# The MLP's down product by one level of Strassen's algorithm, with its weight side on GpSimd

## What is computed

```python
u = jnp.square(jax.nn.relu(_rms_norm(x, g_pre_ffn) @ w_up))
x = x + _rms_norm(u @ w_down, g_post_ffn)
```

## Time and profile before

| | us |
|---|---|
| median of 3 runs (2537.8 to 2539.58) | 2538.49 |
| the profiled execution, its own time | 2545.82 |
| its span, first to last instruction | 2544.0 |
| TensorE busy | 2479.0 (97%) |
| VectorE busy | 1157.3 (45%) |
| ScalarE busy | 674.2 (27%) |
| GpSimd busy | 491.4 (19%) |
| mean granted clock of TensorE | 0.987 |

### The profile page before, as it was taken

How to read it: one execution, slowest core, us unless ns; L and a number is a source line. 1 busy time by engine, 2 the same in 40 slices (tenths; PEclk the granted TensorE clock), 3 DMA queues, 4 the chain that set the end, 5 groups by cost and what they waited for, 6 DMA issues and landing times.

```text
span 2544.0 us, 37470 instructions
## 1 busy us (share of the span) xinstructions
PE 2479.0 (97%) x14264; PEld 2358.0 (93%) x14264; DVE 1157.3 (45%) x2297; ACT 674.2 (27%) x1365; POOL 491.4 (19%) x729
## 2 busy tenths in 40 slices
PE   6999999999999999999999999999999999999998
PEld 6999999999999999999999999988899898898996
DVE  4053424324276666566657435555343343333335
ACT  5222232323222222222222323333121131131221
POOL 1021211102164455445436000001000000000000
PEclk8999999999999999999999999999999999999999
DMA  4251625343333313313323633222021021110114
GB/s 150 90 191 64 225 81 196 103 166 117 121 102 124 117 66 132 123 65 119 127 88 113 216 125 130 93 99 85 17 67 39 27 66 33 33 58 25 50 41 157
DMA packets 219182, 256.88 MB, mean 101 GB/s; under 512 B 8256, under 2 KB 186816, under 8 KB 218944
## 3 DMA queue, kind: packets, MB, share of 16 engines
q1 hardware_dynamic: 219072, 255.37, 30.4%
HBM read 175.12 MB, written 80.22 MB: 100 GB/s over the span
## 4 chain that ended last, share of the span: by engine, by line
PE 72%; issue 12%; DVE 11%; DMA 2%; POOL 2%; ACT 1%; SPq 0%; DVEq 0%; POOLq 0%; ACTq 0%
PE bank L593 10%; PE bank L595 10%; PE bank L594 10%; PE bank L823 5%; PE bank L825 5%; PE bank L824 5%; PE bank L893 5%; PE bank L892 5%; PE bank L894 5%; PE bank L744 3%; DVE QE L1374 2%; DVE PP L1377 2%; PE bank L851 1%; PE bank L853 1%; PE bank L852 1%
## 5 line engine op out<-in xcount | busy, mean ns | idle before, releaser
L593 PE MATMUL bank<-XH,WHI 128*128 128x384 f32 x2304 | 792.9, 344 | 14.3 <-DVE WLO L1209 5.5
L595 PE MATMUL bank<-XH,WLO 128*128 128x384 f32 x2304 | 775.8, 337 | 0.0
L594 PE MATMUL bank<-XL,WHI 128*128 128x384 f32 x2304 | 775.6, 337 | 0.0
L593 PEld LDWEIGHTS bank<-XH,WHI 128*128 128x128 f32 x2304 | 437.6, 190 | 20.4 <-ACT ZST L908 7.1
L594 PEld LDWEIGHTS bank<-XL,WHI 128*128 128x128 f32 x2304 | 437.5, 190 | 0.9
L595 PEld LDWEIGHTS bank<-XH,WLO 128*128 128x128 f32 x2304 | 436.6, 190 | 0.0
L908 ACT ACTIVATE ZST<-bank 128x384 f32<-128x384 f32 x240 | 117.9, 492 | 575.4 <-PE bank L595 573.7
L823 PE MATMUL bank<-XH,WHI 128*128 128x384 f32 x768 | 257.7, 335 | 3.6 <-ACT XH L908 3.6
L825 PE MATMUL bank<-XH,WLO 128*128 128x384 f32 x768 | 257.2, 335 | 0.0
L824 PE MATMUL bank<-XL,WHI 128*128 128x384 f32 x768 | 257.2, 335 | 0.0
L1209 DVE TENSOR_TENSOR WLO<-WRAW,WHI 128x1024 fp32r<-128x1024 f32 x128 | 157.4, 1230 | 210.7 <-ACT WHI L908 205.5
(11 more groups left out here) (173 smaller groups left out, 3231.0 us busy)
## 6 DMA issues: line engine op xcount, KB each, us to landing
scratch_z<-ZST SPq DMA_DIRECT2D x80, 576.0 KB, 2.8
WRAW<-in_w_in SPq DMA_DIRECT2D x80, 512.0 KB, 3.8
HZ<-scratch_z SPq DMA_DIRECT2D x32, 576.0 KB, 5.2
WRAW<-in_w_up SPq DMA_DIRECT2D x32, 512.0 KB, 4.1
WRAW<-in_w_down SPq DMA_DIRECT2D x32, 512.0 KB, 3.3
MG<-scratch_z SPq DMA_DIRECT2D x16, 576.0 KB, 5.9
ZQ<-scratch_z SPq DMA_DIRECT2D x4, 1152.0 KB, 5.5
ZK<-scratch_z SPq DMA_DIRECT2D x4, 1152.0 KB, 7.8
```

The source lines that it names most:

```text
L593: pe.matmul(psum[c][:, 0:CH], WHI[p][:, k, :], XH[:, k, s], start=(k == 0), stop=False)
L594: pe.matmul(psum[c][:, 0:CH], WHI[p][:, k, :], XL[:, k, s], start=False, stop=False)
L595: last = pe.matmul(psum[c][:, 0:CH], WLO[p][:, k, :], XH[:, k, s], start=False, stop=(k == KT - 1))
```

## The change

The down product of a group becomes one level of Strassen's algorithm (seven products in place of eight, in a form whose sums partly build up in the PSUM banks). U, a group's activations (512 FF by 1024 prompt tokens), is halved in FF (k) and tokens (t), the weights in FF and columns (n). Product i reads one U part and one weight part, each 128 x 2 x 512; four of the operands of each side are sums. Each product runs as four token tiles p of 6 matmuls (bank 3+p); the ninth token tile is multiplied plainly, with 6 matmuls behind each of products 0 to 3 (bank 7).

- TensorE: per group 7 x 4 + 4 = 32 sums of 6 matmuls, 192 in place of 216. Up is unchanged.
- Up's results stay in float32 in U: ReLU by ScalarE, square in place by VectorE; the splits move to the parts (`u_hi` on ScalarE, `u_lo` on VectorE, seven per group, two buffers), with four sums of U parts by VectorE.
- Weights: one semaphore and four loads of w_down rows into WDR per group; the sync queue waits there until the previous group's last weight part is split, and w_up loads of blocks 2 to 4 stand behind. ScalarE copies seven high parts, GpSimd makes four sums and seven low parts, each 128 x 1024.
- VectorE adds 33 banks to ACC per group in place of 18.
- End: order of tiles 8, 0 to 7, with the finishing steps among the last additions; the residual of every second tile is added by GpSimd.

Cut to the core (tables, TensorE, ScalarE, VectorE, GpSimd, sync queue):

```diff
+        U_PART = ((2, 0), None, (2, 0), (0, 0), None, (0, 512), (2, 512))
+        W_PART = ((2, 0), None, (2, 512), (0, 0), None, (0, 512), (2, 0))
+        PH_MM = (5, 10, 15, 20, 24, 28, 32)
+        PH_EV = (0, 5, 9, 14, 19, 23, 27)
+        DN, DE = 32, 31
+        Y_ORDER = (8, 0, 1, 2, 3, 4, 5, 6, 7)
...
+                up_w(g, 1)
+                sp.wait_ge(wc_lo, 7 * g + 1)
+                for k in (2, 3, 0, 1):
+                    sp.dma_start(WDR[:, k, :], a["w_down"][0, bass.ds(g * 512 + k * P, P), :]).then_inc(wd_in, 16)
+                for b in range(2, 4 if last else 5):
+                    up_w(g, b)
...
+                for i in range(7):
+                    us_h, us_l, ws_h, ws_l = USH[i % 2], USL[i % 2], WSH[i % 3], WSL[i % 3]
+                    pe.wait_ge(uc_lo, 7 * g + i + 2)
+                    pe.wait_ge(wc_lo, 7 * g + i + 2)
+                    if i == 0:
+                        pe.wait_ge(dn_ev, DE * g + 1)
+                    for p in range(4):
+                        if i:
+                            pe.wait_ge(dn_ev, DE * g + PH_EV[i - 1] + p + 2)
...
+                        product(psum[3 + p][:, :], lambda k: us_h[:, k, ts], lambda k: us_l[:, k, ts], ws_h, ws_l,
+                                i in (0, 1, 3))
...
             def mlp(g, last):
+                act.wait_ge(uc_lo, 7 * g + 1)
                 for b in range(4):
+                    if b < 3 or not last:
+                        up_hi(g, b + 1)
                     for c in range(NC):
+                        act.wait_ge(mm, NC * NB1 + 12 * g + NC * b + c + 1)
+                        act.activation(U[:, b, c * CH:(c + 1) * CH], psum[c][:, 0:CH], ACT.Relu).then_inc(f_r, 1)
...
+                        if c == 1 and b == 3:
+                            w_hi_part(g, 2)
+                act.wait_ge(f_u, 12 * g + 11)
+                u_hi(g, 0)
+                act.wait_ge(f_u, 12 * g + 12)
+                copy(U8H[:, :, :], U[:, :, TP:T]).then_inc(u8_hi, 1)
+                act.wait_ge(s_ok, 4 * g + 1)
+                u_hi(g, 1)
+                for i in range(5):
...
+                    act.wait_ge(dn, DN * g + PH_MM[i] + 1)
+                    act.wait_ge(s_ok, 4 * g + (3, 3, 3, 4, 4)[i])
+                    u_hi(g, i + 2)
+                    if i < 4:
+                        act.wait_ge(t_ok, 4 * g + (3, 3, 3, 4)[i])
+                        w_hi_part(g, i + 3)
...
+                        squared(g, b, c)
+                        if b == 3 and c == 1:
+                            u_lo(g, 0)
+                a11, a12, a21, a22 = (U[:, k:k + 2, t:t + 512] for t in (0, 512) for k in (0, 2))
+                dve.wait_ge(f_u, 12 * g + 12)
+                dve.tensor_tensor(TU[:, :, :], a21, a22, ALU.add).then_inc(s_ok, 1)
+                dve.wait_ge(u8_hi, g + 1)
+                dve.tensor_tensor(U8L[:, :, :], U[:, :, TP:T], plain(U8H[:, :, :]), ALU.subtract).then_inc(u8_lo, 1)
+                u_lo(g, 1)
+                dve.wait_ge(uc_lo, 7 * g + 3)
+                dve.tensor_tensor(TU[:, :, :], TU[:, :, :], a11, ALU.subtract).then_inc(s_ok, 1)
+                dve.wait_ge(acc0, 1)
+                gather(g, 0, 0)
+                dve.wait_ge(s_ok, 4 * g + 2)
+                dve.tensor_tensor(a12, a12, TU[:, :, :], ALU.subtract).then_inc(s_ok, 1)
+                for p in range(1, 4):
+                    gather(g, 0, p)
+                gather8(g, 0)
+                u_lo(g, 2)
+                gather(g, 1, 0)
...
+                for p in range(4):
+                    gather(g, 5, p)
+                    if p < 3:
+                        y_mean(2 + p)
+                    finish(1 + p)
+                gather(g, 6, 0)
+                gather(g, 6, 1)
+                y_mean(5)
+                gather(g, 6, 2)
+                y_mean(6)
+                finish(5)
+                gather(g, 6, 3)
+                y_mean(7)
+                finish(6)
+                y_mean(8)
+                finish(7)
+                finish(8)
...
             pool.memset(ACC[:, :, :], 0.0).then_inc(acc0, 1)
+            pool.sem_inc(wc_lo, 1)
...
+            with pool.Fori(0, FF // 512) as g:
+                pool.wait_ge(wd_in, 64 * g + 64)
+                pool.wait_ge(wc_lo, 7 * g + 1)
+                pool.tensor_tensor(TB[:, :, :], b12, b11, ALU.subtract).then_inc(t_ok, 1)
+                w_lo_part(g, 0)
+                pool.wait_ge(t_ok, 4 * g + 1)
+                pool.tensor_tensor(b12, b22, b12, ALU.subtract).then_inc(t_ok, 1)
+                w_lo_part(g, 1)
+                w_lo_part(g, 2)
+                pool.wait_ge(wc_lo, 7 * g + 3)
+                pool.tensor_tensor(TB[:, :, :], b22, TB[:, :, :], ALU.subtract).then_inc(t_ok, 1)
+                pool.wait_ge(t_ok, 4 * g + 3)
+                pool.tensor_tensor(b21, b21, TB[:, :, :], ALU.subtract).then_inc(t_ok, 1)
+                for i in range(3, 7):
+                    w_lo_part(g, i)
```

More of the change, by code:

```diff
@@ L527, in _, with up_w @@
             sp.dma_start(x1s[(NT - 1) * P:, :], X1R[(NT - 1) % 2][:, :]).then_inc(x1_st[(NT - 1) % 2], 16)
+            def up_w(g, b):
+                sp.wait_ge(w_lo, W_FFN + 4 * g + b - 1)
+                sp.dma_start(as_block(WRAW[b % 2]), a["w_up"][0, :, bass.ds(g * 512 + b * P, P)]
+                             .rearrange("(k p) n -> p k n", p=P)).then_inc(w_raw[b % 2], 16)
             def mlp_w(g, last):
[L530 to L548, removed]
+                up_w(g, 1)
[4 more added lines that the diff above has]
+                    up_w(g, b)
+            for g in range(FF // 512):
+                mlp_w(g, g == FF // 512 - 1)
             sp.wait_ge(mm, NC * NB1 + 12 * (FF // 512))
@@ L868, in _, with product @@
             pe.wait_ge(d_x1, NT)
+            def product(out, uh, ul, wh, wl, fresh):
+                for k in range(2):
+                    pe.matmul(out, uh(k), wh[:, k, :], start=(fresh and k == 0), stop=False, skip_group_check=True)
+                    pe.matmul(out, uh(k), wl[:, k, :], start=False, stop=False, skip_group_check=True)
+                    last = pe.matmul(out, ul(k), wh[:, k, :], start=False, stop=(k == 1), skip_group_check=True)
+                last.then_inc(dn, 1)
             def mlp(g, first):
@@ L879, in mlp @@
[L879 to L895, removed]
+                for i in range(7):
[7 more added lines that the diff above has]
+                            pe.wait_ge(dn_ev, DE * g + PH_EV[i - 1] + p + 2)
+                        ts = slice(p * P, (p + 1) * P)
+                        product(psum[3 + p][:, :], lambda k: us_h[:, k, ts], lambda k: us_l[:, k, ts], ws_h, ws_l,
+                                i in (0, 1, 3))
+                    if i < 4:
+                        k0 = (2, 0, 2, 0)[i]
+                        if i == 0:
+                            pe.wait_ge(u8_lo, g + 1)
+                        if i in (1, 3):
+                            pe.wait_ge(dn_ev, DE * g + (6 if i == 1 else 15))
+                        product(psum[7][:, :], lambda k: U8H[:, k0 + k, :], lambda k: U8L[:, k0 + k, :], ws_h, ws_l, i != 2)
@@ L1155, in _ @@
             act.wait_ge(w_lo, W_FFN + 1)
-            def mlp(g, last):
[L1158 to L1171, removed]
+            for i in range(2):
+                act.wait_ge(x1_st[i], 16 * ((NT + 1 - i) // 2))
@@ L1190, in _ @@
             mlp(NG - 1, True)
[L1192 to L1197, removed]
+            for j in range(1, NT):
+                y_square(j)
         @block.vector
@@ L1555, in mlp, with finish @@
-            def mlp(g, last):
[L1556 to L1564, removed]
+            def finish(j):
+                t = Y_ORDER[j]
+                dve.wait_ge(y_rs, j + 1)
+                if j >= 2:
+                    dve.wait_ge(y_st[j % 2], 16 * (j // 2))
+                dve.wait_ge(gb_in, 32)
+                last = dve.scalar_tensor_tensor(OF[j % 2][:, :], ACC[:, t, :], yrs[:, t:t + 1], GF[:, :], ALU.mult, ALU.mult)
+                if j % 2:
+                    last.then_inc(y_mul, 1)
+                    return
+                ch(last)
+                dve.wait_ge(x1_in[0], 16 * (j // 2 + 1))
+                dve.tensor_tensor(OF[0][:, :], OF[0][:, :], X1F[0][:, :], ALU.add).then_inc(y_ok[0], 1)
@@ L1575, in mlp @@
[L1575 to L1588 removed]
+                        if c == 0 and (b < 3 or not last):
+                            up_lo(g, b + 1)
@@ new lines, in mlp @@
+                gather(g, 4, 0)
+                gather(g, 4, 1)
+                y_mean(0)
+                gather(g, 4, 2)
+                gather(g, 4, 3)
+                finish(0)
+                u_lo(g, 6)
+                y_mean(1)
+                for p in range(4):
+                    gather(g, 5, p)
[5 more added lines that the diff above has]
+                y_mean(5)
@@ L1591, in _ @@
             mlp(NG - 1, True)
-            finish(NT - 1)
         @block.gpsimd
```

169 lines of the change are left out of this document (113 added, 56 removed).

## The result

| | before | after |
|---|---|---|
| median of 8 runs each (us) | 2539.17 (2537.28 to 2543.37) | 2556.94 (2550.55 to 2563.22) |
| profiled execution, span | 2545.8, 2544.0 | 2557.9, 2556.1 |
| TensorE resumes ahead of the MLP's third up piece | 1748.85 | 1745.03 |
| from there to the end of the span | 795.2 | 811.1 |

The changed kernel takes 1.0071 of the time before, [1.0061, 1.008]: 17.8 us more by the medians, at a forecast of 18.0. The stages ahead of the MLP have the same code. (All nine traces of changed kernels lie between these two, and the one trace of before at 1748.8 outside, so this is not shown.) So I compare from that resumption on: **+15.9 us**.

What follows compares the result with a forecast made beforehand. TensorE, busy 97% of the span, was taken as the bound. -43.5 + 28.3 + 12.8 + 1.7 + 2.6 + 4.2 + 11.9 = +18.0: 2563.8 us profiled, 2556.5 median; 8 in 10 within 2535 to 2578.

Steps and rivals of the forecast that it cites:

- A: Rival: GpSimd and VectorE don't hold each other up, border wait 3.02 us; 2548 us, chance 0.11.
- B: Rival: A holds and TensorE's clock stays full too; 2535.5 us, no change, chance 0.10.
- C: Rival: first parts are ready when the down product begins, so wait and half clock go; 2514 us, chance 0.09.
- D: Rival, heavier: half clock lasting 6.8 us, or a slower matmul pitch; 10 to 14 us more, 2569, chance 0.12.
- my clause that GpSimd might hold VectorE before product 1: Proviso to C: if GpSimd still holds VectorE there, some of the removed time comes back; no size given.
- matmuls: Down product: 24 of 216 matmuls fewer per group at 0.2267 us each, in 8 groups 43.5 us saved.
- border: From up to down product: TensorE waits 3.54 us per group for VectorE's first low part; 28.3 us.
- clock or queue, product 2: Behind each border: half clock for 3.41 us or VectorE's queue, 12.8 us; product 2 waits 0.2 per group, 1.7.
- first group: w_down loads wait for GpSimd's memset, delaying block 2 of w_up; TensorE waits 2.6 us (0 to 6).
- last group: Finishing steps among VectorE's additions make product 6 wait for its banks: 0.4 + 3.6 + 0.2 = 4.2 us.
- tail: From TensorE's end to the span's end: 22.4 us of finishing and store against 10.45, 11.9 more (5 to 15).
- Nothing for: Zero cost claimed for extra additions, products 1 to 6's low parts, ScalarE's time, GpSimd's 27 us and DMA bytes.

Runs made afterwards that it cites:

- early: Changed kernel with ScalarE's weight high parts 1 and 2 taken two and three pieces earlier, so GpSimd finishes sooner; 2544.36 us, 1.0029 of before.
- early_keepbusy: early plus 12 unused 512-column matmuls between the last up piece and product 0; 2537.48 us, 0.999 of before.
- memwait: Changed kernel with GpSimd waiting for its own memset before raising the semaphore that releases the w_down loads; 2558.63 us, 1.0075 of before.
- both: Changed kernel with the moves of early and order together; 2517.11 us, 0.9919 of before.
- order: Changed kernel with ScalarE's first high part of U put ahead of the group's last ReLU; 2556.03 us, 1.0073 of before.
- small: Changed kernel with GpSimd's weight sums and low parts done on one column only, the rest left out; 2544.55 us, 1.0026 of before.
- keepbusy: Changed kernel with 12 unused 512-column matmuls between the last up piece and product 0; 2555.46 us, 1.0059 of before.

## Why the prediction was right, and where it was not

The forecast (2556.5, slower) came out, by the mechanism it named, and the rivals fell: A on the 1.66 and 2.73 of VectorE beside GpSimd; B with A, and on the half clock in five groups (*early* and *early_keepbusy* show that in its world a full clock does save 1.6 us at each fall); C on the 3.30 at the border; D on the pitch, which held, and on falls of 3.41 (one of 6.8 came in *memwait*, with a group of 99.6). C's world is *both*, with 2517.1 where I had worked out 2514: when the first parts are ready, the kernel is faster. But C's condition as I wrote it, ScalarE's order alone, is *order*, which brought nothing; my clause that GpSimd might hold VectorE before product 1 was the whole answer. By steps:

| term | predicted | measured | from |
|---|---|---|---|
| matmuls | -43.5 | -43.5 | pitch 0.2267 held |
| border | 28.3 | 27.8 | 8 x (3.64 - 0.17) |
| clock or queue, product 2 | 12.8 + 1.7 | 15.2 | 8 x (98.82 - 49.92 - 43.53 - 3.47) |
| first group | 2.6 | 0 | no wait |
| last group | 4.2 | 5.6 | 3.6 + 0.35 + half clock 1.6 |
| tail | 11.9 | 11.2 | 21.9 - 10.7 |
| sum | 18.0 | 16.3 | against 15.9 |

That the medians differ by 17.8, within 0.2 of the forecast, is in part luck: the trace has 15.9, and in it a term of 2.6 that did not come and one mis-sized by 1.4 stand against each other.

- **The border** was right in each part; *early* and *small* show the 3.02 without GpSimd (3.03), and the 0.44 that its third sum adds.
- **The clock.** "Either the clock or this queue takes some 1.6, not both" was right as a price and half right as an event: I had the half clock in all eight groups, it came in five, and the queue took the same in the other three. The wait before product 1 is 0.95 idle, 1.1 lost, where I had 1.4.
- **The first group** is the step that failed: "the sync queue now waits, before the four w_down loads, for GpSimd's memset". The raise stands behind the memset in the program, but went out at its start. With the wait forced, the term was there to 0.05.
- **The last group** was mis-sized: I priced product 6's wait for its banks at 3.6 (3.60 lost) and forgot the half clock behind it, which I had counted at the borders.
- **The tail** had GpSimd's hold (3.22) as predicted; GpSimd's waits for the two X1F buffers were not in my list, and other steps were shorter.
- **Nothing for** GpSimd's time, the extra additions and the DMA: right in the seven groups before the last, as *both* shows with TensorE busy throughout.

Of the 43.5 us saved, the borders and what follows them took 43.0, so that nothing was left against the last group and the tail, 16.8 us, which are the measured loss. *both* gives back all of the borders' part but some 5 us in the eight groups (94.1 against 93.45).

## To carry to other kernels

When a change turns a streamed operand into one with a late last piece, write down the queue of each engine from the last matmul ahead of the border to the first behind it, because two engines' orders may have to change together before either shows a gain. A wait moved is not a wait removed: *order* cut the border by 2.3 us and returned them 6 and 10 us later. Matmuls put into a wait to keep the clock full pay only where nothing else waits behind it (*early_keepbusy*, not *keepbusy*). GpSimd was busy 28% of the time and still cost some 11 us, by where its operations lay beside VectorE's; move them before taking them away.

## What the runs showed of the hardware

- **Which borders halve the clock** is not told by the length of the wait: with 3.30 idle (3.22 in the first group) five of eight in after and two in *memwait* (one of them for 6.8 us), with 2.87 (2.78) idle every second one in *early* and five in *small*. In *order* it halved in four groups behind a wait of 1.94 to 2.02, itself behind one of 1.0 and one of 0.8. A fall of 3.41 us costs 1.6 us (98.2 against 96.6). Why the others are spared stays open.
- **A semaphore raised by GpSimd's queue behind a memset** (1745.01) doesn't wait for the memset to end (1752.78). Only a wait on the memset's own semaphore does that (1748.11 behind 1748.03).
- **GpSimd and VectorE take turns** by whole instructions: VectorE's 0.56 became 2.73 (after), its 1.23 became 3.31 (*order*), and GpSimd's sum, 2.35 alone, 3.38 (*order*). VectorE's additions with one operand in PSUM stayed at 0.67 to 0.69 (256 of them in after). The Trainium skill (SBUF — State Buffer, "SBUF: two separate sides") calls the shared port pair an exclusive lock, held for the whole instruction; the rows agree, in both directions.
- **After a wait** the first matmul is followed by the second after 0.33, not 0.2267 (1890.47 and 1890.80 in after, still at the full clock). Two such steps in a group of half clock and four in the others make 0.2 to 0.4 us that my sum didn't have.
